# Division of the neighbourhood and banded probabilities by their sums, moved from VectorE to GpSimd

## The chip, the core and the metric

The kernel runs on one core of one Trainium2 chip. A core has TensorE (matrix products and transposes, results in PSUM), VectorE and ScalarE (element by element, in SBUF and PSUM), GpSimd (element by element, in SBUF) and SyncE, which issues DMA transfers. The engines run their own instruction lists side by side and wait for each other by semaphores. The metric is the device time of one execution in microseconds (us), lower is better.

## What is computed

Two transformer blocks in sequence over 512 tokens and 16 meta tokens of width 1024, in float32. The first has a feed-forward part, a mixer of stick-breaking attention and a recurrent part, and a second feed-forward part. The second block has a feed-forward part, three attention mixers side by side, a gated merge and a feed-forward part. The change touches two of these three mixers:

```python
# neighborhood_attention, 8 heads, a grid of 64 columns, meta keys always visible
p = jax.nn.softmax(jnp.concatenate([sm, s], axis=-1), axis=-1).astype(v.dtype)
p_nb = p[..., N_META:].reshape(bsz, H, GRID_W, wr, GRID_W)
return (jnp.einsum("bhcm,bmhd->bchd", p[..., :N_META], vm)
        + jnp.einsum("bhcxy,bxyhd->bchd", p_nb, v_nb))

# window_gqa, 8 query heads, 2 key heads, |i-j| <= 128, one sink logit per head
def sink_softmax(s, sink):
    m = jnp.maximum(jnp.max(s, axis=-1, keepdims=True), sink)
    e = jnp.exp(s - m)
    return e / (jnp.sum(e, axis=-1, keepdims=True) + jnp.exp(sink - m))
```

The third one (differential attention over all positions) has its own normalisation, which is left as it is.

## The kernel before

Nearly all of the time goes into products of weights and activations on TensorE, each in three passes (high by high, low by high, high by low part). The stage that matters here is `pe_mixers`, `act_mixers` and `dve_mixers`: attention of the second block.

**Units.** `mixer_units` lists 48 units: 16 of kind a (differential, 4 heads by 4 blocks of 128 queries), then 32 that alternate b (neighbourhood) and c (banded): `(b, p, i), (c, p, i)` for 4 head pairs p and 4 query blocks i. A b or c unit treats two heads x = 0, 1. Its probabilities of one head are 16 meta columns and 128 per key block: 272 columns for b and for c with i = 0 and 3, 400 columns for c with i = 1 and 2 (`blocks_of`). They lie in the tile P, of which six slots go round, two for a unit (`p_slot`), so a unit's slots are taken again by the unit three places on.

**Order.** `mixer_order` makes each engine's list. In round r an engine does, for each of its steps, the unit that lies so many places back:

```python
STEPS = {"PE": [(3, "turn"), (4, "values"), (0, "scores")],
         "ACT": [(3, "pt"), (1, "exp"), (5, "square"), (5, "yh")],
         "DVE": [(5, "out"), (1, "soft"), (2, "join"), (5, "yl")]}
```

For a b or c unit the steps follow on each other like this:
- scores (TensorE, L2825): four products for the two heads into PSUM, with 256 or 384 key columns and 16 meta columns.
- soft (VectorE, `dve_soft`, L2896 for b, L2906 and L2913 for c): a custom instruction that adds the bias to the scores, writes them negated into P and keeps the minimum in STAT. For c a small sum for the sink follows (L2917).
- exp (ScalarE, L2850): exponential in place in P, with the sum over the columns into STAT; for c also that of the sink (L2853).
- join (VectorE): for c the sink is added to the sum (L2951), then the reciprocal of both sums (L2954, semaphore a_inv), and two instructions that multiply the probabilities of each head by it (L2957, semaphore a_scl).
- turn (TensorE, L2777 and L2781): the transposes of P into PSUM, one of the meta columns and four or six of the key blocks. It waits for the unit's a_scl.
- pt (ScalarE, L2839 or L2841, L2844): copies them to SBUF. values (TensorE, L2796 and L2801): products with the values.
- yh, yl (ScalarE L2867 and L2870, VectorE L2973 and L2978): once per head pair, high and low part of the result, out of PSUM.

VectorE's list in a round with softmax of a c unit is thus L2906, L2913, L2917, then the join of the b unit before it; in the other kind of round L2896, then the join of the c unit before it. `mixer_counts` works out at which count of a semaphore each event of each unit stands.

**GpSimd** has a list of its own, `pool_program`: sums of squares (`pool_squares`), products in the recurrent part, fills and some DMA transfers (`pool_project_2`). Semaphore names of the second block go on counting on semaphores of the first (`GOES_ON`), so that the order of instructions shows a_inv as s_rho, a_scl as s_bonus, a_sum as s_sb_scan and a_exp as s_sb_keep.

Of the kernel before, what the change touches and what calls it, by code (L numbers as in the profile page):

```python
# [21 lines left out]
ALU = mybir.AluOpType  # L22
# [158 lines left out]
class Weights:  # L181
# [57 lines left out]
    def order_loads(self, dram):  # L239
# [13 lines left out]
        for i, item in enumerate(self.items):  # L253
# [20 lines left out]
            else:  # L274
# [17 lines left out]
       "lt", "half", "pm", "corner", "ks", "rs", "solved", "sa", "updated", "outs", "grown", "state", "yb",  # L292
       "y_hi", "y_lo",        "rowc", "lam",
              "hank0", "hank1", "rpb0", "rpb1", "rpb2", "bias",
       "v_moved", "v_turn", "a_min", "a_sink", "a_sq", "f_scl", "pad"])


GOES_ON = {"m1": ("lora", 8), "m2": ("knorm", 5), "gated": ("rkb", 4), "a_z": ("sb_z", 24),
# [70 lines left out]
def mixer_order(units, engine):  # L369


    return [(units[r - late], step) for r in range(len(units) + 5) for late, step in STEPS[engine]
            if 0 <= r - late < len(units)]


def mixer_counts(units):


    count, made = {}, {}

    def event(name, *keys):
        made[name] = made.get(name, 0) + 1
        for key in keys:
            count[name, key] = made[name]

    for u, step in mixer_order(units, "PE"):
        kind, h, i = u
        heads = kind in ("a", "b", "c")
        if step == "scores" and kind == "a":
            event("a_z", (u, 0))  # L390
        if step == "scores" and heads:
            event("a_z", (u, 1))
        if step == "turn":
            event("a_turn", u)
        if step == "values" and heads:
            event("a_val", u)
    for u, step in mixer_order(units, "ACT"):
        kind, h, i = u
        heads = kind in ("a", "b", "c")
        if step == "pt" and heads:  # L400
            event("a_pt")
            event("a_pt", u)
        if step == "exp" and heads:
            event("a_exp", (u, 0))
            event("a_exp", (u, 1))
            if kind == "c":
                event("a_sexp", u)
        if step == "square" and kind == "a":
            event("a_sq", u)
        if step == "yh" and kind in ("b", "c") and i == 3:  # L410
            event("yh", (4 if kind == "b" else 8) + h)
    for u, step in mixer_order(units, "DVE"):
        kind, h, i = u
        if step == "out" and kind == "a":
            event("a_y", u)
        if step == "soft" and kind in ("a", "b", "c"):
            if kind in ("a", "c"):
                event("a_min", (u, 0))
                event("a_min", (u, 1))
            event("a_sum", (u, 0))  # L420
            event("a_sum", (u, 1))
            if kind == "c":
                event("a_sink", u)
        if step == "join" and kind in ("a", "b", "c"):
            if kind == "c":
                event("a_den", u)
            event("a_inv", u)
            if kind == "a":
                event("a_nl", u)
            else:  # L430
                event("a_scl")
            event("a_scl", u)
        if step == "yl" and kind in ("b", "c") and i == 3:
            event("yl", (4 if kind == "b" else 8) + h)
    return count


def build(nc, dram, out):
    ctx = ExitStack()
    with ctx:  # L440
        S = {name: ctx.enter_context(nc.semaphore("s_" + name)) for name in SEMAPHORES}
# [365 lines left out]
        units = mixer_units()  # L807
        count = mixer_counts(units)
# [183 lines left out]
        def pool_squares(e, q, s, R, end=DT):  # L992
            for k in range(1, end):
                slot, _ = tmp_of["sq", s, k]
                q.wait_ge("sq", DT * s + k + 1)
                q.wait_ge("acc", ACC_BASE[s] + k - 1)
                e.tensor_tensor(tcols(ACC, R), tcols(ACC, R), tcols(TMP[:, slot, :], R),
                                ALU.add).then_inc(S["acc"], 1)
# [1698 lines left out]
        def p_slot(u):  # L2697
            return 2 * place_of[u] % 6

        def probs(u, x):  # L2700

            kind, h, i = u
            if kind == "a":
                return P[:, p_slot(u) + x, :]
            total = NM + 128 * blocks_of(u)
            return P[:, p_slot(u):p_slot(u) + 2, :].rearrange("p a n -> p (a n)")[:, x * total:(x + 1) * total]
# [25 lines left out]
        def stat(u, field, x, n=1):  # L2732
            return STAT[:, place_of[u] % 6, field, x:x + n]
# [25 lines left out]
        def pe_mixers(e, q):  # L2759
# [3 lines left out]
            for u, step in mixer_order(units, "PE"):  # L2763
                kind, h, i = u
                heads = kind in ("a", "b", "c")
                if step == "turn" and heads:
                    slot, n = p_slot(u), blocks_of(u)
                    q.wait_ge("a_scl", count["a_scl", u])
                    q.wait_ge("a_pt", 2 * place_of[u])
                    if kind == "a":  # L2770
                        e.transpose(PS[0:NM, 5, 384:512], P[:, slot, 0:NM], cst("ident"))
                        for y in range(n):
                            last = e.transpose(PS[:, 4, 128 * y:128 * y + 128],
                                               P[:, slot, NM + 128 * y:NM + 128 * y + 128], cst("ident"))
                    else:
                        both = P[:, slot:slot + 2, :].rearrange("p a n -> p (a n)")
                        e.transpose(PS[0:2 * NM, 5, 384:512], both[:, 128 * n:128 * n + 2 * NM], cst("ident"))  # L2777
                        for x in range(2):
                            for y in range(n):
                                bank, c = (4, 2 * x + y) if kind == "b" else (4 + x, y)  # L2780
                                last = e.transpose(PS[:, bank, 128 * c:128 * c + 128],  # L2781
                                                   probs(u, x)[:, parts_of(u, x)[0]][:, 128 * y:128 * y + 128],
                                               cst("ident"))
                    last.then_inc(S["a_turn"], 1)
# [139 lines left out]
        def dve_mixers(e, q):  # L2924
# [3 lines left out]
            for u, step in mixer_order(units, "DVE"):  # L2928
                kind, h, i = u
# [17 lines left out]
                if step == "join" and kind in ("b", "c"):  # L2947
                    q.wait_ge("a_exp", count["a_exp", (u, 1)])
                    if kind == "c":
                        q.wait_ge("a_sexp", count["a_sexp", u])  # L2950
                        e.tensor_tensor(stat(u, 2, 0, 2), stat(u, 2, 0, 2), stat(u, 3, 0, 2),  # L2951
                                        ALU.add).then_inc(S["a_den"], 1)
                        q.wait_ge("a_den", count["a_den", u])
                    e.reciprocal(stat(u, 4, 0, 2), stat(u, 2, 0, 2)).then_inc(S["a_inv"], 1)  # L2954
                    q.wait_ge("a_inv", count["a_inv", u])
                    for x in range(2):
                        e.tensor_scalar(probs(u, x), probs(u, x), stat(u, 4, x), None, ALU.mult).then_inc(S["a_scl"], 1)  # L2957
                if step == "yl" and u == units[-2]:
                    q.wait_ge("a_turn", 47)
                    q.wait_ge("a_sum", count["a_sum", (units[-1], 1)])  # L2960
# [8 lines left out]
                if step == "yl" and kind in ("b", "c") and i == 3:  # L2969
                    k = (4 if kind == "b" else 8) + h  # L2970
                    q.wait_ge("yh", count["yh", k])
                    if kind == "b":
                        e.tensor_tensor(YL[:, k, :].rearrange("p (r c) -> p c r", r=8),  # L2973
                                        out_bank_of(kind).rearrange("p (c r) -> p c r", r=8),
                                        YH[:, k, :].bitcast(F32).rearrange("p (r c) -> p c r", r=8),
                                        ALU.subtract).then_inc(S["yl"], 1)
                    else:
                        e.tensor_tensor(YL_C[:, h, :], out_bank_of(kind), YH[:, k, :].bitcast(F32),  # L2978
                                        ALU.subtract).then_inc(S["yl"], 1)

        def sync_strip(e, q, kind, h):
            s = h if kind == "a" else 4 + h
# [148 lines left out]
        def pool_program(e):  # L3131
            q = Waits(e, S)
            e.memset(FILLER, 1.0).then_inc(S["filled"], 1)
            q.wait_ge("load", 32)
            q.wait_ge("cst", 16)
            pool_squares(e, q, 1, FULL)
            pool_prepare(e, q)
            pool_breaking(e, q)
            pool_rwkv(e, q)
            pool_squares(e, q, 2, REAL, 4)  # L3140
            q.wait_ge("sq", 3 * DT)
            q.wait_ge("n_lo", 3 * DT)
            e.dma_start(X[:, :, 0:NM], dram["meta_2"]).then_inc(S["small"], 16)
            pool_to_meta(e, q)
            pool_squares(e, q, 5, FULL)
            pool_project_2(e, q)
            pool_squares(e, q, 6, REAL, 4)
            pool_squares(e, q, 7, REAL, DT - 1)

# [193 lines left out]
```

## Time and profile before

| | us |
|---|---|
| median of 3 runs | 2491.49 |
| lowest, highest | 2490.38, 2491.88 |
| span of the profiled execution | 2486.8 |
| TensorE busy | 2440.2 (98%) |
| VectorE busy | 1705.4 (69%) |
| ScalarE busy | 1081.3 (43%) |
| GpSimd busy | 98.2 (4%) |

The span is that of the instructions of one profiled execution; the times of the runs have what lies around it too. In the rows below a time is counted from the start of the span. In a timeline a row is: start, duration, engine, line of the kernel, operation, output<-input, shape, count, and in brackets how long the engine had been idle before and what ended that. PE is TensorE's products, PEld its weight loads, DVE is VectorE, ACT ScalarE, POOL GpSimd. A matmul's end is modelled, so a round on TensorE is best read from start to start.

### The profile page before, as it was taken

The page shows a single profiled execution, that of the slowest core. Times are in us where ns is not written, and L with a number is a line of the kernel's source. Part 1 is how long each engine was busy: PE and PEld are TensorE (multiplying, and loading weights), DVE is VectorE, ACT ScalarE, POOL GpSimd, SP SyncE. Part 2 cuts the span into 40 slices and gives each one's busy share as a digit, 9 for nine tenths or more (in the row PEclk, how much of TensorE's full clock was granted, in tenths as well). Part 3 has the DMA queues.
Part 4 walks back from the last instruction along what each step waited for, and adds up shares of the span by engine and source line. Part 5 has one row for each costly group of instructions (what it writes and reads, how often), then busy time and mean ns, then how long its engine had stood idle before and what let it go on. Part 6 is the DMA issues. An engine that isn't in the chain of part 4 may idle for free.

```text
span 2486.8 us, 49060 instructions
## 1 busy us (share of the span) xinstructions
PE 2440.2 (98%) x20460; PEld 2245.9 (90%) x20460; DVE 1705.4 (69%) x2926; ACT 1081.3 (43%) x1959; POOL 98.2 (4%) x108
## 2 busy tenths in 40 slices
PE   9999999999999999999999999999989999999998
PEld 7999999996887989898999999898867888989896
DVE  6878675646656879688879684242976445879694
ACT  5444343334434535356535253112874324535352
POOL 0000001000320000001000002000000000000001
PEclk8999999999999999998999999999999999999999
DMA  4233333220001333332233333232212333233322
GB/s 148 85 107 102 102 95 90 81 80 11 4 13 44 103 111 98 107 103 85 73 115 106 99 93 97 71 93 76 55 48 76 92 96 101 100 102 103 102 90 72
DMA packets 72379, 213.01 MB, mean 86 GB/s; under 512 B 12796, under 2 KB 20028, under 8 KB 72032
## 3 DMA queue, kind: packets, MB, share of 16 engines
q1 hardware_dynamic: 70496, 209.03, 26.7%
q8 instruction: 163, 2.67, 0.4%
q0 software_dynamic: 480, 0.73, 0.1%
q14 instruction: 56, 0.46, 0.1%
q10 hardware_dynamic: 1184, 0.12, 0.0%
HBM read 207.61 MB, written 2.20 MB: 84 GB/s over the span
## 4 chain that ended last, share of the span: by engine, by line
PE 87%; DVE 7%; ACT 4%; issue 2%; DVEq 0%; POOL 0%; ACTq 0%; POOLq 0%
PE PS L863 21%; PE PS L1398 20%; PE PS L1355 11%; PE PS L1356 11%; PE PS L1357 11%; DVE WL L948 1%; PE PS L1233 1%; ACT WH L936 1%; PE PS L1706 1%; PE PS L1707 1%; PE PS L1705 1%; PE PS L1319 1%; PE PS L2256 1%; DVE P L2888 1%; PE PS L2825 1%
## 5 line engine op out<-in xcount | busy, mean ns | idle before, releaser
L1355 PE MATMUL PS<-OPH,WH 128*128 128x256 f32 (+1 forms) x2112 | 606.4, 287 | 3.1 <-DVE OPL L1105 2.7
L1357 PE MATMUL PS<-OPH,WL 128*128 128x256 f32 (+1 forms) x2112 | 601.8, 285 | 0.0
L1356 PE MATMUL PS<-OPL,WH 128*128 128x256 f32 (+1 forms) x2112 | 600.2, 284 | 0.0
L936 ACT ACTIVATE WH<-WR 128x1024 fp32r<-128x1024 f32 (+2 forms) x277 | 275.5, 995 | 564.0 <-PE PS L863 272.6
L948 DVE TENSOR_TENSOR WL<-WR,WH 128x1024 fp32r<-128x1024 f32 (+2 forms) x277 | 318.7, 1151 | 191.1 <-ACT WH L936 191.0
L1355 PEld LDWEIGHTS PS<-OPH,WH 128*128 128x128 f32 x2112 | 403.5, 191 | 6.5 <-DVE OPL L1105 3.0
L1356 PEld LDWEIGHTS PS<-OPL,WH 128*128 128x128 f32 x2112 | 403.5, 191 | 2.1 <-issue 1.7
L1357 PEld LDWEIGHTS PS<-OPH,WL 128*128 128x128 f32 x2112 | 402.7, 191 | 0.0
L936 ACT ACTIVATE WH<-SUMS 128x512 fp32r<-128x512 f32 x352 | 211.1, 623 | 229.8 <-DVE SUMS L974 186.6
L948 DVE TENSOR_TENSOR WL<-SUMS,WH 128x512 fp32r<-128x512 f32 x352 | 234.1, 684 | 21.5 <-ACT WH L936 21.2
L863 PE MATMUL PS<-NHI,WH 128*128 128x264 f32 (+2 forms) x960 | 234.5, 309 | 1.5 <-ACT TMP L2623 1.0
L863 PE MATMUL PS<-NLO,WH 128*128 128x264 f32 (+2 forms) x960 | 232.9, 308 | 0.0
L863 PE MATMUL PS<-NHI,WL 128*128 128x264 f32 (+2 forms) x960 | 232.1, 307 | 0.0
L863 PEld LDWEIGHTS PS<-NHI,WH 128*128 128x128 f32 x960 | 154.9, 189 | 13.7 <-issue 1.6
L863 PEld LDWEIGHTS PS<-NLO,WH 128*128 128x128 f32 x960 | 156.1, 189 | 8.7
L863 PEld LDWEIGHTS PS<-NHI,WL 128*128 128x128 f32 x960 | 155.6, 189 | 8.3
L1398 PE MATMUL PS<-HH_A,WH 128*128 128x264 f32 (+1 forms) x572 | 152.3, 320 | 0.0
L1398 PE MATMUL PS<-HL_A,WH 128*128 128x264 f32 (+1 forms) x572 | 152.3, 321 | 0.0
L1398 PE MATMUL PS<-HH_A,WL 128*128 128x264 f32 (+1 forms) x572 | 151.9, 320 | 0.0
L1530 DVE TENSOR_TENSOR T<-PS,RT 128x528 f32<-128x528 f32 (+1 forms) x64 | 44.8, 699 | 148.1 <-PE PS L1398 148.1
L1398 PE MATMUL PS<-HH_B,WH 128*128 128x264 f32 (+1 forms) x476 | 127.1, 321 | 0.0
L1398 PE MATMUL PS<-HL_B,WH 128*128 128x264 f32 (+1 forms) x476 | 126.5, 321 | 0.0
(472 smaller groups left out, 4670.3 us busy)
## 6 DMA issues: line engine op xcount, KB each, us to landing
WR<-in_ffn_up SPq DMA_DIRECT2D x64, 512.0 KB, 3.9
WR<-in_ffn_down SPq DMA_DIRECT2D x64, 512.0 KB, 3.7
WR<-in_ffn_gate SPq DMA_DIRECT2D x56, 512.0 KB, 3.7
WR_MORE<-in_ffn_gate SPq DMA_DIRECT2D x32, 512.0 KB, 4.5
WR_MORE<-in_ffn_up SPq DMA_DIRECT2D x24, 512.0 KB, 4.4
WR<-in_ffn_down SPq DMA_DIRECT2D x32, 384.0 KB, 3.3
WR<-in_w_gate SPq DMA_DIRECT2D x24, 512.0 KB, 3.6
WR<-in_w_out SPq DMA_DIRECT2D x16, 512.0 KB, 3.6
```

The source lines that it names most:

```text
L863: last = e.matmul(bank, left[:, cols], right[:, a:b] if right.shape[1] == L else right, start=(kt == 0 and left is wh and right is hi), st ...
L936: e.activation(split_unit(i)[0][:, 0:w], src, ACT.Copy).then_inc(S["w_hi"], 1)
L948: e.tensor_tensor(lo[:, 0:w], src, hi[:, 0:w].bitcast(F32), ALU.subtract).then_inc(S["w_lo"], 1)
L1233: last = e.matmul(at[:, i:i + 1], data[:, a:a + 128], cst("ones", 128, 1), start=opens, stop=k == DT - 1, skip_group_check=True)
L1319: e.matmul(PS[:, 3, :], FILLER[:, 0:128], FILLER, start=True, stop=True, skip_group_check=True)
L1355: e.matmul(o, wh[:, at:at + 128], hi, start=k == 0 and s in (1, 2, 5), stop=False, skip_group_check=True)
L1356: e.matmul(o, wh[:, at:at + 128], lo, start=False, stop=False, skip_group_check=True)
L1357: last = e.matmul(o, wl[:, at:at + 128], hi, start=False, stop=k == 3, skip_group_check=True)
L1398: last = e.matmul(bank, left[:, cols], right[:, a:b], start=t == first and left is wh and right is hi, stop=t == end - 1 and left is wl, s ...
L1530: e.tensor_tensor(tcols(t, R), pcols(pair_of["down", f, c, m][0], R), tcols(RT, R), ALU.mult).then_inc(S["d_t"], 1)
L1705: e.matmul(o, NHI[:, kt, a:a + 128], wh[:, c], start=kt == 0, stop=False)
L1706: e.matmul(o, NHI[:, kt, a:a + 128], wl[:, c], start=False, stop=False)
```

## The change

The two multiplications leave VectorE's join for the kinds b and c and are made by GpSimd, in a new loop over the units, `pool_mixers`, which stands in GpSimd's list behind `pool_project_2` and ahead of the sums of squares. It waits for each unit's reciprocal. They count on a new semaphore, shared, for which the turn of a b or c unit now waits; a units keep a_scl.

```diff
-       "v_moved", "v_turn", "a_min", "a_sink", "a_sq", "f_scl", "pad"])
+       "v_moved", "v_turn", "a_min", "a_sink", "a_sq", "f_scl", "pad", "shared"])
@@ mixer_counts
             if kind == "a":
                 event("a_nl", u)
+                event("a_scl", u)
             else:
-                event("a_scl")
-            event("a_scl", u)
+                event("shared")
+                event("shared", u)
@@ pe_mixers
-                    q.wait_ge("a_scl", count["a_scl", u])
+                    scaled = "a_scl" if kind == "a" else "shared"
+                    q.wait_ge(scaled, count[scaled, u])
@@ dve_mixers
                     e.reciprocal(stat(u, 4, 0, 2), stat(u, 2, 0, 2)).then_inc(S["a_inv"], 1)
-                    q.wait_ge("a_inv", count["a_inv", u])
-                    for x in range(2):
-                        e.tensor_scalar(probs(u, x), probs(u, x), stat(u, 4, x), None, ALU.mult).then_inc(S["a_scl"], 1)
@@ new
+        def pool_mixers(e, q):
+            for u in units:
+                if u[0] == "a":
+                    continue
+                q.wait_ge("a_inv", count["a_inv", u])
+                for x in range(2):
+                    e.tensor_scalar(probs(u, x), probs(u, x), stat(u, 4, x), None, ALU.mult).then_inc(S["shared"], 1)
@@ pool_program
             pool_project_2(e, q)
+            pool_mixers(e, q)
             pool_squares(e, q, 6, REAL, 4)
```

VectorE's list before, from the softmax of the first 384-column c unit (ISA rows are the custom instruction and the read of its minimum) to the join of the b unit and the next softmax (line numbers after the change are two higher):

```order
L2913 ISA P,STAT<-PS,HANK,STAT 128x384 [waits s_a_min]
L2913 ISA STAT 128x1
L2917 TENSOR_TENSOR STAT<-STAT,SM 128x2 [waits s_sb_scan]
L2954 RECIPROCAL STAT<-STAT 128x2 [waits s_sb_keep]
L2957 TENSOR_SCALAR P<-P,STAT 128x272 [waits s_rho]
L2957 TENSOR_SCALAR P<-P,STAT 128x272
L2896 ISA P,STAT<-PS,BIAS 128x272 [waits s_rpb2,s_sb_turn,s_sb_z]
```

The same place after the change:

```order
L2915 ISA P,STAT<-PS,HANK,STAT 128x384 [waits s_a_min]
L2915 ISA STAT 128x1
L2919 TENSOR_TENSOR STAT<-STAT,SM 128x2 [waits s_sb_scan]
L2956 RECIPROCAL STAT<-STAT 128x2 [waits s_sb_keep]
L2898 ISA P,STAT<-PS,BIAS 128x272 [waits s_rpb2,s_sb_turn,s_sb_z]
```

The reciprocal is the last of the join now, and the next softmax stands right behind it.

GpSimd's list after the change, around the new loop's start; before, the row behind the fill of BIAS was the first sum of squares:

```order
L2682 MEMSET PT 128x2x128 [waits s_w_used]
L2683 MEMSET BIAS 128x3x32
L2986 TENSOR_SCALAR P<-P,STAT 128x272 [waits s_rho]
L2986 TENSOR_SCALAR P<-P,STAT 128x272
L2986 TENSOR_SCALAR P<-P,STAT 128x272 [waits s_rho]
```

Each pair waits for its unit's reciprocal (s_rho), the 32 pairs in the order of the units.

TensorE's list before, one round (transposes, values, scores) and the start of the next:

```order
L2777 MATMUL PS<-CST,P 32x128 [waits s_sb_pt,s_bonus]
L2781 MATMUL PS<-CST,P 128x128 x4
L2796 MATMUL PS<-PT,VMB 128x128 [waits s_rk]
L2801 MATMUL PS<-PT,VC 64x128 x4
L2825 MATMUL PS<-QK_128 128x384 [waits s_sb_scan]
```

And after:

```order
L2779 MATMUL PS<-CST,P 32x128 [waits s_sb_pt,s_shared]
L2783 MATMUL PS<-CST,P 128x128 x4
L2798 MATMUL PS<-PT,VMB 128x128 [waits s_rk]
L2803 MATMUL PS<-PT,VC 64x128 x4
L2827 MATMUL PS<-QK_128 128x384 [waits s_sb_scan]
```

Nothing moves on TensorE; the turn waits for GpSimd's semaphore in place of VectorE's. Values and scores still stand behind it.

## Rows read from the trace of the kernel before

**Rows 1.** The page's first part: engine, busy us (share of the span), instructions.

```profile
PE 2440.2 (98%) x20460; PEld 2245.9 (90%) x20460; DVE 1705.4 (69%) x2926; ACT 1081.3 (43%) x1959; POOL 98.2 (4%) x108
```

**Rows 2.** Timeline of two rounds, TensorE's first transpose (L2777) and VectorE.

```profile
1800.01 0.28 PE L2777 MATMUL PS<-CST,P 128*32 128x128 f32 x1
...
1801.05 0.17 DVE L2954 RECIPROCAL STAT<-STAT 128x2 f32<-128x2 f32 x1
...
1802.45 0.28 PE L2777 MATMUL PS<-CST,P 128*32 128x128 f32 x1
...
1802.57 0.23 DVE L2906 CUSTOM_DVE_ANT_0 P<-PS,HANK,NSINK 128x16 f32<-128x16 f32 x1 [0.69 <-PE PS L2825]
...
1803.89 0.16 DVE L2954 RECIPROCAL STAT<-STAT 128x2 f32<-128x2 f32 x1
...
1804.08 0.63 DVE L2957 TENSOR_SCALAR P<-P,STAT 128x272 f32<-128x272 f32 x2
```

**Rows 3.** Timeline of a round with a 384-column c unit, the same engines.

```profile
1787.53 0.28 PE L2777 MATMUL PS<-CST,P 128*32 128x128 f32 x1
...
1789.23 0.16 DVE L2954 RECIPROCAL STAT<-STAT 128x2 f32<-128x2 f32 x1
...
1790.11 0.28 PE L2777 MATMUL PS<-CST,P 128*32 128x128 f32 x1 [0.29 <-DVE P L2957]
```

**Rows 4.** The scaling's line L2957: count, ns min/median/max, first and last start, shapes.

```profile
L2957 DVE TENSOR_SCALAR P<-P,STAT x64: 353/361/429, 1783.9 to 1870.7; 128x272 f32<-128x272 f32 x48, 128x400 f32<-128x400 f32 x16
```

**Rows 5.** Timeline behind the end of a head pair, VectorE and TensorE's next transpose.

```profile
1812.07 0.69 DVE L2978 TENSOR_TENSOR YL_C<-PS,YH 128x512 fp32r<-128x512 f32 x1 [0.49 <-ACT YH L2870]
...
1813.59 0.17 DVE L2954 RECIPROCAL STAT<-STAT 128x2 f32<-128x2 f32 x1
...
1814.80 0.28 PE L2777 MATMUL PS<-CST,P 128*32 128x128 f32 x1
```

**Rows 6.** Timeline of GpSimd: fills and additions of different widths.

```profile
398.52 0.58 POOL L2009 MEMSET CHANNELS<- 128x576 f32 x1 [1.65 <-PE PS L863]
...
520.20 1.22 POOL L2128 MEMSET RENEW<- 128x1344 f32 x1 [119.25 <-PE PS L1905]
...
641.59 0.72 POOL L2417 TENSOR_TENSOR SMALL<-NB,CST 128x256 f32<-128x256 f32 x1 [2.73 <-PE PS L2256]
642.45 0.73 POOL L2417 TENSOR_TENSOR TMP<-NB,CST 128x256 f32<-128x256 f32 x1
...
775.21 1.41 POOL L997 TENSOR_TENSOR ACC<-ACC,TMP 128x512 f32<-128x512 f32 x1 [45.04 <-ACT TMP L990]
```

**Rows 7.** Timeline: VectorE hands over to GpSimd, and GpSimd to TensorE.

```profile
617.32 0.69 DVE L2365 TENSOR_TENSOR NB<-PS,CST 128x512 f32<-128x512 f32 x1 [0.33 <-PE PS L2206]
...
618.17 0.72 POOL L2417 TENSOR_TENSOR SMALL<-NB,CST 128x256 f32<-128x256 f32 x1 [11.19 <-DVE NB L2365]
...
2468.90 1.29 POOL L997 TENSOR_TENSOR ACC<-ACC,TMP 128x512 f32<-128x512 f32 x1 [4.29 <-ACT TMP L990]
2470.25 0.52 PEld L1624 LDWEIGHTS PS<-CST,ACC 128*128 128x128 f32 x4 [0.19 <-POOL ACC L997]
```

**Rows 8.** Timeline of the last unit: its reciprocal and its first transpose.

```profile
1870.18 0.17 DVE L2954 RECIPROCAL STAT<-STAT 128x2 f32<-128x2 f32 x1
...
1871.06 0.28 PE L2777 MATMUL PS<-CST,P 128*32 128x128 f32 x1 [0.16 <-DVE P L2957]
```

**Rows 9.** Windows: busy us of PE, PEld, DVE, ACT, POOL; granted clock; DMA.

```profile
1785.00:1870.00 85.00, 77.18 (x733) 61.65 (x731) 64.46 (x308) 62.54 (x208) 0.00 (x0) 0.96 0.19 49
...
1834.00:1841.00 7.00, 6.89 (x36) 5.08 (x37) 4.55 (x21) 2.66 (x8) 0.00 (x0) 0.51 0.12 39
```

**Rows 10.** Timeline: an addition on GpSimd while VectorE runs a two-input one.

```profile
637.58 0.69 DVE L2377 TENSOR_TENSOR TU<-TU,CST 128x512 f32<-128x512 f32 x1
...
637.67 1.19 POOL L2417 TENSOR_TENSOR TMP<-NB,CST 128x256 f32<-128x256 f32 x1
```

## The prediction

> **What bounds the kernel now.** First the page's busy shares and its chain: TensorE is busy 2440.2 of 2486.8 us and GpSimd 98.2 us [rows 1], so only what makes TensorE wait longer, or less, can move the time. The change touches one stage alone, the 32 neighbourhood (b) and banded (c) units between about 1782 and 1872 us. Over 1785 to 1870 TensorE is busy 77.18 of 85.00 us, VectorE 64.46, ScalarE 62.54, GpSimd nothing, at a mean granted clock of 0.96 [rows 9]. So TensorE sets the pace there too, but with little to spare around it, and the timeline has to be read for how much.
>
> In that stage each engine goes through the units in turn. A TensorE round is the transposes of unit u-3 ("turn"), the value products of u-4 and the scores of u. The scores start VectorE's softmax part of u, behind which stands "join" of u-1: a reciprocal of the sums, then two scalings of the probabilities. They let TensorE's next turn start. I count everything from the start of a turn.
>
> A free round is 2.44 us of TensorE work: the turn of 1800.01 is followed by the one of 1802.45 without a wait [rows 2]. VectorE's part of a round has two kinds:
> - X: softmax of a c unit, then join of a b unit. With the 256-column c unit the softmax starts 0.12 us after the turn and the reciprocal ends at 1804.05, 1.60 us after it; two scalings follow, and VectorE had waited 0.69 us for the scores [rows 2]. The next turn could start about 2.3 us after the last one, so TensorE does not wait. With the 384-column c unit the reciprocal ends at 1789.39, 1.86 us after the turn of 1787.53, and the next turn comes at 1790.11, after 2.58 us: 0.14 us late, with an idle TensorE ended by the scaling [rows 3].
> - Y: softmax of a b unit, then join of a c unit: the reciprocal ends at 1801.22, 1.21 us after its turn [rows 2], with 1.2 us left.
>
> So the scaling sits on a path with 0.1 us of slack in half of the X rounds and none in the other half. There are 16 X rounds, 8 of each width.
>
> **What is removed.** 64 VectorE instructions, 48 of 272 columns and 16 of 400, 353 to 429 ns each [rows 4]. A pair of 272 columns takes 0.63 us from first start to last end [rows 2]. That makes some 22 us of VectorE time free, and buys nothing by itself: VectorE's next softmax waits for TensorE's scores in these rounds, not for VectorE.
>
> **What is added.** 64 GpSimd scalings, in pairs, with a handoff at each side. GpSimd has nothing else to do here: the row before them in its queue is the fill of BIAS, and the sums of squares behind them belong to a later stage, so it is queued behind nothing and holds up nothing. What is queued behind the longer wait is TensorE's whole round.
>
> Handoffs: VectorE's NB ends at 618.01 and the GpSimd instruction that waits for it starts at 618.17, 0.16 us; GpSimd's ACC ends at 2470.19 and TensorE's load starts at 2470.25, 0.06 us. Together 0.22 us [rows 7].
>
> One scaling: the trace has no GpSimd instruction with one tensor read and one written, so I bound it. Below, a fill, which only writes: 0.58 us for 576 columns and 1.22 us for 1344, so 0.83 ns a column and 0.10 fixed, which gives 0.33 us for 272. Above, an addition, which reads two: 0.72 us for 256 and 1.41 us for 512 columns, 2.70 ns a column, which gives 0.76 us for 272 and 1.08 for 400. Two additions behind each other have 0.14 us between them [rows 6]. A scaling reads one and writes one, between the two, and neither row is nearer; I take the middle, 0.55 us for 272 and 0.76 us for 400 (fill 0.43). A pair is then 2 x 0.55 + 0.14 = 1.24 us, for 400 columns 1.66. From the reciprocal's end to the next turn it takes H = 0.22 + 1.24 = 1.46 us instead of 0.72.
>
> **The sum.** X with 256: 1.60 + 1.46 = 3.06 against 2.44, 0.62 us more. X with 384: 1.86 + 1.46 = 3.32 against 2.58, 0.74 more. Y with 400 columns: 1.21 + 0.22 + 1.66 = 3.09 from its turn, also over 2.44, but it costs nothing more: a late turn delays the scores behind it, and these feed the turn after the next, so that of two rounds in succession one pays; two rounds take 2.44 plus the larger of the two latencies. The next larger is X's each time.
>
> Three times, where a head pair ends, VectorE also makes the low part of the output (YL_C) ahead of a Y round, and that round starts late: its reciprocal ends at 1813.76 and the next turn comes at 1814.80 [rows 5]. With 0.22 + 1.66 = 1.88 it would come at 1815.64, 0.84 later, 0.10 beyond the 0.74 that the X round before has already cost. Three times: 0.3 us.
>
> At the end, the last unit's reciprocal ends at 1870.35 and its turn starts at 1871.06 [rows 8]; all that follows up to the gates hangs on it: 1.46 - 0.71 = 0.75 us.
>
> 8 x 0.62 + 8 x 0.74 + 0.3 + 0.75 = 11.9 us. After this stage TensorE is the bound again and gives nothing back. Against the profiled execution that is 2486.8 + 11.9 = 2498.7 us of span; the median of the runs lies 4.7 us above that span, so 2491.5 + 11.9 = **2503.4 us**.
>
> **Rivals.**
> Not slower: GpSimd scales at the rate of its fills and with no gap. H = 0.22 + 0.66 = 0.88: X with 256 costs 1.60 + 0.88 - 2.44 = 0.04, with 384 0.16, the end 0.17: 1.8 us, 2493.3 us, within what can be told from no change (0.2%, 5 us). The point that decides: 8 (H - 0.84) + 8 (H - 0.72) + (H - 0.71) = 17H - 13.2 reaches 5 us at H = 1.07, a pair of 0.85 us. For it: one read stream may cost no more than none. Against it: each scaling also fetches its factor per partition, and the addition costs over three times the fill. The Trainium skill ("GPSIMD Engine Reference", 4.1 Engine selection) says that two-input operations are about twice as slow there as on VectorE and one-input ones roughly at line rate; by that this rival would hold. The trace shows the first half (0.72 us for 256 columns) and nothing for the second.
>
> Two-read rate: the scaling costs what the addition does. Pair 1.66, H = 1.88: X 1.04 and 1.16, the three ends of head pairs 0.32 more each (2.52 us from 1813.76), the last one 1.17: 8 x 1.04 + 8 x 1.16 + 1.0 + 1.2 = 19.8 us, 2511.3 us.
>
> The clock: TensorE's granted clock was 0.51 over 1834 to 1841, some rounds behind the end of the second head pair; those 7 us did the work of about 3.5. That alone takes the mean of the 85 us to 0.96, so it was 1.0 in all the rest, behind the two other ends too [rows 9]. With more idle time in every second round, two more such stretches are possible: up to 7 us on top, around 2509 us. For it: the waits get longer. Against it: two of the three ends left the clock alone.
>
> Contention: an addition on GpSimd took 1.19 instead of 0.73 us while VectorE ran one with both inputs in SBUF [rows 10]. If VectorE's softmax instruction of the next unit, which runs while GpSimd scales, did the same, a scaling would take 1.01 us, a pair 2.16, H = 2.38: 17 x 2.38 - 13.2 + 0.3 = 27.6 us, 2519 us. Against it: that instruction reads PSUM and one SBUF operand. By the Trainium skill ("SBUF — State Buffer", Who interferes with whom) a VectorE instruction with at most one SBUF input outside its two-port modes does not contend with GpSimd; by that this rival falls away, and it leaves contention only at the end, where VectorE's NHI and NLO instructions run.
>
> A gain would need a pair plus its handoffs under 0.72 us, below two fills alone (0.66) with handoffs; only a low-clock stretch that happens not to occur could then bring some 2 us.
>
> **How the numbers follow.** Forecast (one scaling of 272 columns between 0.40 and 0.70 us, so H from 1.16 to 1.76 and 2498 to 2508 us) 0.57; fill rate 0.15; two-read rate 0.13; clock on top 0.08; contention 0.05; other 0.02. The range 2495 to 2514 leaves out the lower half of the fill case, contention and the clock on top of the dearer cases, under 0.2 together. Slower by over 0.2%: forecast, two-read, clock, contention and a little of the fill case, 0.84; within 0.2%: 0.13; faster 0.03.
>
> **What would show it.** In the profile after: GpSimd busy about 98 + 48 x 0.55 + 16 x 0.76 = 137 us; TensorE's first transpose of a unit idle before it in every X round, ended by GpSimd's P, about 10 us more in total; turns at distances of 2.44 and about 3.1 or 3.3 us in alternation; VectorE idle for longer before its softmax; the stages before and after of the same length; the gates start some 12 us later. I am wrong if a scaling lasts under 0.4 us (then TensorE hardly waits), if turns come late in both kinds of round, or if the low clock lasts longer than 7 us in this stage.

## The result, and the profile after

The changed kernel takes 2512.39 us (median of 4 runs, 2511.45 to 2516.51) against 2490.94 us before: 1.0094 times, 95% interval 1.0082 to 1.0106. It is slower by some 22 us. The forecast was 2503.4 us: the right direction, and about half of the size.

The page after. Columns are busy us, share of the span, instructions:

```profile
span 2509.4 us, 49060 instructions
...
PE 2444.1 (97%) x20460; PEld 2247.0 (90%) x20460; DVE 1685.9 (67%) x2862; ACT 1080.8 (43%) x1959; POOL 164.1 (7%) x172
```

Beside [rows 1], VectorE lost 19.5 us and 64 instructions, GpSimd gained 65.9 us and 64 instructions. The forecast had GpSimd at 137 us. The line of the new instructions, with shortest, median and longest duration in ns:

```profile
L2986 POOL TENSOR_SCALAR P<-P,STAT x64: 952/964/1287, 1783.7 to 1892.0; 128x272 f32<-128x272 f32 x48, 128x400 f32<-128x400 f32 x16
...
  DVE STAT L2956: 93.5, 27
...
  PEld PS L2779: 24.2, 22
  PE PS L2779: 21.6, 20
```

A scaling of 272 columns lasts 0.95 to 0.97 us in 47 of 48 cases (the last one of all 1.13), one of 400 columns 1.28 or 1.29; [rows 4] had 0.35 to 0.43 us on VectorE. TensorE's first transposes now wait 21.6 us for them. Before, they waited 2.5 us for the scalings on VectorE (the same view of L2957):

```profile
  PE PS L2777: 2.5, 6
```

One X round after, with a 256-column c unit, the counterpart of [rows 2]; the timeline of TensorE's first transpose (L2779 now), the reciprocal (L2956) and GpSimd:

```profile
1802.75 0.28 PE L2779 MATMUL PS<-CST,P 128*32 128x128 f32 x1
...
1804.11 0.16 DVE L2956 RECIPROCAL STAT<-STAT 128x2 f32<-128x2 f32 x1
1804.36 1.90 POOL L2986 TENSOR_SCALAR P<-P,STAT 128x272 f32<-128x272 f32 x2 [1.67 <-DVE STAT L2956]
...
1806.32 0.28 PE L2779 MATMUL PS<-CST,P 128*32 128x128 f32 x1 [1.06 <-POOL P L2986]
...
1808.76 0.28 PE L2779 MATMUL PS<-CST,P 128*32 128x128 f32 x1
```

The reciprocal ends at 1804.27, 1.52 us after the turn ("turn" always means the start of a unit's first transpose); GpSimd starts 0.09 us later, works 1.90 us on the pair without a gap, and the turn comes 0.06 us behind it: 2.05 us from the reciprocal to the turn, where the forecast had 1.46. The next distance, 1808.76 - 1806.32, is 2.44 us again: every second round pays, as forecast.

The chain of waits there, from the reciprocal ahead of one late turn to the start of the softmax ahead of the next; each piece is start, us, what:

```profile
1804.11 0.17 DVE STAT L2956
1804.28 0.08 issue
1804.36 1.91 POOL P L2986 x2
1806.27 0.04 issue
1806.32 0.28 PE PS L2779
1806.60 0.44 PE PS L2783 x4
1807.04 0.22 PE PS L2798 x2
1807.26 0.81 PE PS L2803 x12
1808.07 0.78 PE PS L2827 x8
1808.85 0.03 issue
1808.88 0.23 DVE P L2908
```

This is the circle that now sets the pace of the stage: one TensorE round, the softmax, the reciprocal, both scalings, and only then the next late turn. In between lies the turn that is on time.

The stage by a window, in the columns of [rows 9]:

```profile
1782.00:1894.00 112.00, 86.00 (x777) 68.64 (x775) 49.09 (x264) 65.22 (x219) 66.13 (x64) 0.92 0.14 40
```

The granted clock over the stage went from 0.96 [rows 9] to 0.92. Taken in windows of 1 us, it was low (0.5) for 17.1 us in four stretches, against 6.8 us in one before. From the first turn of a b unit to the turn of the last c unit it is 107.58 us (1785.65 to 1893.23) against 86.28 (1784.78 to 1871.06 [rows 8]): 21.3 of the 22.6 us by which the span grew. The first turn comes 0.87 us later too, since the first scalings stand ahead of it.

### The profile page after: what moved, and what is told of

It reads as the page before. It is cut to its first block, busy times and chain, and to the rows that moved or that the text cites. A ratio compares the mean times of both kernels' runs of the same rounds, so it can differ in the third digit from the quotient of the medians.

```text
span 2509.4 us, 49060 instructions
## 1 busy us (share of the span) xinstructions
PE 2444.1 (97%) x20460; PEld 2247.0 (90%) x20460; DVE 1685.9 (67%) x2862; ACT 1080.8 (43%) x1959; POOL 164.1 (7%) x172
## 4 chain that ended last, share of the span: by engine, by line
PE 86%; DVE 7%; ACT 4%; issue 2%; POOL 1%; DVEq 0%; ACTq 0%; POOLq 0%
PE PS L864 20%; PE PS L1399 20%; PE PS L1356 11%; PE PS L1357 10%; PE PS L1358 10%; DVE WL L949 1%; POOL P L2986 1%; ACT WH L937 1%; PE PS L1707 1%; PE PS L1708 1%; PE PS L1706 1%; PE PS L1320 1%; PE PS L1234 1%; PE PS L2257 1%; DVE P L2890 1%
## 5 line engine op out<-in xcount | busy, mean ns | idle before, releaser
L949 DVE TENSOR_TENSOR WL<-SUMS,WH 128x512 fp32r<-128x512 f32 x352 | 234.6, 686 | 21.9 <-ACT WH L937 21.6
L998 POOL TENSOR_TENSOR ACC<-ACC,TMP 128x528 f32<-128x528 f32 (+1 forms) x26 | 39.3, 1511 | 1401.2 <-ACT TMP L991 1401.2
```

The costliest lines, as they stand in the source:

```text
L949: e.tensor_tensor(lo[:, 0:w], src, hi[:, 0:w].bitcast(F32), ALU.subtract).then_inc(S["w_lo"], 1)
```

## The experiments

My theory after the result: the time from the reciprocal to the turn is the whole cost, it went from 0.72 to 2.05 us because of what the scaling takes on GpSimd, and of two rounds one pays. Rivals: each scaling pays for itself in its own round; the handoffs over a third engine cost, not the instructions; VectorE's work beside it slows GpSimd; the low clock carries a good part.

The table has all kernels but the one in which the forms of instruction are timed by themselves. "Turns" is the time from the first to the last of the 32 turns of the profile, of one execution each; "low" is the time at half clock in the stage. The kernel before was measured again beside each series: 2490.94 us beside the change, 2490.53 beside the next four rows, 2489.94 beside "the change, waits filled" and "before, three waits filled", and 2490.29 beside the other three. Differences are taken within a series.

| kernel | median us | to before (95% interval) | turns us | low us |
|---|---|---|---|---|
| before | 2489.9 to 2490.9 | | 86.28 | 6.8 |
| the change | 2512.4 | 1.0094 (1.0082 to 1.0106) | 107.58 | 17.1 |
| b units alone | 2515.15 | 1.0093 (1.0078 to 1.0108) | 108.84 | 23.9 |
| c units alone | 2505.27 | 1.0055 (1.0039 to 1.0072) | 102.74 | 10.2 |
| one head each | 2495.82 | 1.0022 (1.0012 to 1.0033) | 94.20 | 10.2 |
| one multiplication for both heads | 2495.52 | 1.0020 (1.0011 to 1.0030) | 92.13 | 6.8 |
| one head each, as a multiplication | 2490.46 | 1.0005 (0.9995 to 1.0014) | 88.07 | 6.8 |
| the change, waits filled | 2509.67 | 1.0074 (1.0059 to 1.0089) | 105.10 | 0.0 |
| b units alone, waits filled | 2504.54 | 1.0060 (1.0046 to 1.0074) | 101.03 | 0.0 |
| before, three waits filled | 2487.87 | 0.9992 (0.9983 to 1.0002) | 83.84 | 0.0 |
| the same, second series | 2487.47 | 0.9990 (0.9981 to 0.9999) | 83.81 | 0.0 |

### Half of the change: b units, c units

```diff
 # mixer_counts, pe_mixers: the turn of the other kind waits for a_scl again (left out here)
 # pool_mixers
-                if u[0] == "a":
+                if u[0] != "b":          # the other kernel: != "c"
 # dve_mixers, join: VectorE keeps the other kind
+                    if kind != "b":
+                        q.wait_ge("a_inv", count["a_inv", u])
+                        for x in range(2):
+                            e.tensor_scalar(probs(u, x), probs(u, x), stat(u, 4, x), None, ALU.mult).then_inc(S["a_scl"], 1)
```

> GpSimd scales the b units only, VectorE the c units as before. Theory (latency, one of two rounds pays): with 2.05 us from the reciprocal's end to the next turn, as in the profile after, the X rounds pay 8 x (1.60 + 2.05 - 2.44) + 8 x (1.86 + 2.05 - 2.58) = 20.3 us, nearly all of the change's 21.5 us, so about 2511 us. Rival (each scaling pays for itself, in every round): half of it, about 2502 us.

> GpSimd scales the c units only. Theory: the Y rounds, which had 1.2 us left, pay alone: 8 x (1.21 + 2.05 - 2.44) + 8 x (1.21 + 0.15 + 2.57 - 2.58) + 1.5 = 18.9 us, about 2510 us, so that this and the b half sum to some 39 us where both together cost 21.5. Rival (each pays for itself): about 11 us, 2502 us, and the two halves sum to the whole.

Measured: 24.6 us more for the b half and 14.7 for the c half, 39 us together, where the whole costs 21.5. The rival by which each scaling pays for itself falls: it needed halves of 11. That the sum also meets the theory's 39 is partly luck, for the halves missed it in opposite directions: the b half came out 4.3 us above its theory (2515.15 for 2511), which the section on the clock takes up, and the c half 4.2 us below (14.7 for 18.9). In the c half's profile the rounds into the three ends of head pairs fell from 4.42 to 3.61 us, which the theory did not count. The turns with the c units alone on GpSimd (the reading of the other half stands with its filled version, below):

```profile
1798.62 0.28 PE L2782 MATMUL PS<-CST,P 128*32 128x128 f32 x1
1802.59 0.28 PE L2782 MATMUL PS<-CST,P 128*32 128x128 f32 x1 [1.45 <-POOL P L2993]
1805.03 0.28 PE L2782 MATMUL PS<-CST,P 128*32 128x128 f32 x1
```

3.97 us for the round that waits for a pair of 400 columns (3.93 by the theory) and 2.44 for the next. In the changed kernel both kinds of round are late at times, and two rounds with 256-column softmax keep their sum:

```profile
1832.21 0.28 PE L2779 MATMUL PS<-CST,P 128*32 128x128 f32 x1 [0.71 <-POOL P L2986]
1835.08 0.28 PE L2779 MATMUL PS<-CST,P 128*32 128x128 f32 x1 [0.36 <-POOL P L2986]
1837.91 0.28 PE L2779 MATMUL PS<-CST,P 128*32 128x128 f32 x1 [0.32 <-POOL P L2986]
1841.17 0.28 PE L2779 MATMUL PS<-CST,P 128*32 128x128 f32 x1 [0.97 <-POOL P L2986]
```

2.83 + 3.26 = 6.09 us, which is 2.44 + 3.65, the free round and the late one. Waits in every round do not mean that every round pays.

### One head each

```diff
+                    e.tensor_scalar(probs(u, 0), probs(u, 0), stat(u, 4, 0), None, ALU.mult).then_inc(S["a_scl"], 1)   # VectorE
-                for x in range(2):
-                    e.tensor_scalar(probs(u, x), probs(u, x), stat(u, 4, x), None, ALU.mult).then_inc(S["shared"], 1)
+                e.tensor_scalar(probs(u, 1), probs(u, 1), stat(u, 4, 1), None, ALU.mult).then_inc(S["shared"], 1)   # GpSimd
 # left out: the counts, and the turn's wait, which is for both a_scl and shared now
```

> VectorE scales the first head of each b and c unit, GpSimd the second at the same time. Theory (the length of the GpSimd instructions is the cost): from reciprocal to turn 0.09 + 0.96 + 0.06 = 1.11 us, 8 x (1.60 + 1.11 - 2.44) + 8 x (1.86 + 1.11 - 2.58) + 0.4 = 5.7 us, 2497 us. Rival (what costs is the handoff over a third engine, or the low clock, whatever the length): more than half of the change's cost stays, over 2502 us.

Measured: 5.3 us more (2495.82 against 2490.53, interval 3.0 to 8.2 us), where 5.7 were expected; in the profile the turns take 7.9 us more. With about half of GpSimd's work gone, three quarters of the cost (by the medians) or two thirds (by the turns) are gone, so neither handoffs nor a third engine as such are the main price. The scaling itself was slower, though:

```profile
1800.02 0.16 DVE L2956 RECIPROCAL STAT<-STAT 128x2 f32<-128x2 f32 x1
...
1800.21 0.36 DVE L2958 TENSOR_SCALAR P<-P,STAT 128x272 f32<-128x272 f32 x1
...
1800.27 1.13 POOL L2987 TENSOR_SCALAR P<-P,STAT 128x272 f32<-128x272 f32 x1 [1.97 <-DVE STAT L2956]
...
1801.50 0.27 PE L2779 MATMUL PS<-CST,P 128*32 128x128 f32 x1 [0.41 <-issue]
```

1.13 instead of 0.96 us while VectorE scales the other head, in all 24 of that width (1127 ns is the shortest). From the reciprocal to the turn that makes 1.32 us in place of the expected 1.11, for which the prediction's line 17H - 13.2 gives 9.2 us; so the close hit of the median owes something to luck. In the changed kernel, where VectorE's custom instructions run beside the scalings, nothing of the kind happens: 952 ns shortest, 964 ns median. The Trainium skill ("SBUF — State Buffer", Who interferes with whom) counts a scaling on VectorE among the instructions that can take the port pair it shares with GpSimd; the trace agrees, with 0.17 us more for GpSimd's scaling.

### One multiplication for both heads

```diff
-                for x in range(2):
-                    e.tensor_scalar(probs(u, x), probs(u, x), stat(u, 4, x), None, ALU.mult).then_inc(S["shared"], 1)
+                ...   # both: the two slots of P as 128 x 2 x total, total = 16 + 128 per key block
+                by = stat(u, 4, 0, 2).unsqueeze(2).broadcast_to([128, 2, total])
+                e.tensor_tensor(both, both, by, ALU.mult).then_inc(S["shared"], 1)
```

> GpSimd scales both heads with one two-input multiplication whose second input repeats the two factors. Theory: at 2.70 ns a column, as its additions of the kernel before, 544 columns take 1.47 us in place of 1.90, H = 1.62, 17 x 1.62 - 13.2 = 14.3 us, about 2505 us, 7 us under the change. Rival (the form makes no difference, or the repeated operand costs as much as the factor of the scaling): 2512 us.

Measured: 5.0 us more (2495.52 against 2490.53). That is 16.5 us less than the change costs, where 7 less were expected. One instruction does both heads in 1.09 us, where the scaling takes 0.96 for one:

```profile
1800.50 0.16 DVE L2955 RECIPROCAL STAT<-STAT 128x2 f32<-128x2 f32 x1
...
1800.74 1.09 POOL L2988 TENSOR_TENSOR P<-P,STAT 128x544 f32<-128x544 f32 x1 [1.90 <-DVE STAT L2955]
...
1801.89 0.09 PEld L2778 LDWEIGHTS PS<-CST,P 128*32 128x32 f32 x1 [0.41 <-POOL P L2988]
1801.89 0.28 PE L2778 MATMUL PS<-CST,P 128*32 128x128 f32 x1 [0.31 <-POOL P L2988]
```

From the reciprocal's end (1800.66) to the turn 1.23 us, which is 17 x 1.23 - 13.2 = 7.7 us by the prediction's own line; the turns grew by 5.9. The columns are the same to the last one; what differs is the form of the instruction, and that there is one for two. The next run takes these two apart.

### The forms by themselves

```diff
+            for form in ("scalar_272", "scalar_400", "scalar_800", "number_272", "copy_272", "add_272", "spread_272",
+                         "spread_544"):
+                ...   # tensor_scalar with stat-like factor; with 1.5; tensor_copy; tensor_tensor of two tiles (ALU.mult);
+                      # tensor_tensor with one column repeated; with two columns repeated, 272 times each
```

> The kernel before, with 24 GpSimd instructions on a scratch tile in a stretch in which GpSimd idles (after the fill of VMB at 1612 us), three of each form. Theory (an instruction of this form costs this by itself): the scaling with a factor per partition takes 0.95 us for 272 columns and 1.28 for 400 here too; 800 columns 2.3 us. Rival (VectorE's softmax slows it in the changed kernel): 0.5 to 0.6 us for 272 here. The other forms tell what is dear: a plain number as factor, a copy, a multiplication of two tiles (0.76 by the additions), and one with a repeated factor, of 272 and of 544 columns.

This kernel was executed once. The third round of them, in GpSimd's timeline; the first row stands for the scaling of 272 columns alone, from a narrower window:

```profile
1636.08 0.96 POOL L2681 TENSOR_SCALAR ROWS<-ROWS 128x272 f32<-128x272 f32 x1
```

```profile
1641.38 0.89 POOL L2683 TENSOR_SCALAR ROWS<-ROWS 128x272 f32<-128x272 f32 x1
1642.33 0.41 POOL L2685 COPY ROWS<-ROWS 128x272 f32<-128x272 f32 x1
1642.83 0.78 POOL L2687 TENSOR_TENSOR ROWS<-ROWS 128x272 f32<-128x272 f32 x1
1643.69 0.64 POOL L2689 TENSOR_TENSOR ROWS<-ROWS 128x272 f32<-128x272 f32 x1
```

On a scratch tile, far from the stage, the scaling takes the same 0.96 us for 272 columns, 1.28 for 400 and 2.29 for 800, as the theory had it; with a plain number 0.89, so the factor per partition is not what is dear. A copy of the same columns takes 0.41: one read and one write are cheap, close to the fill rate (0.33). The multiplication of two tiles takes 0.78, as the additions said (0.76), and the one with a repeated factor 0.64. The scaling is the dearest of the five, dearer than the form that reads twice as much. So in the changed kernel too it is the form that makes it slow, and not what runs beside it.

These are the undisturbed rows. Six of the 24 took longer, and each of these began while VectorE ran L948, which makes the low part of the weights (two inputs in SBUF, 128x1024). The first scaling of 272 columns took twice its time:

```profile
1614.44 1.23 DVE L948 TENSOR_TENSOR WL<-WR,WH 128x1024 fp32r<-128x1024 f32 x1
1614.53 1.97 POOL L2681 TENSOR_SCALAR ROWS<-ROWS 128x272 f32<-128x272 f32 x1
```

### One head each, with the cheap form

```diff
-                e.tensor_scalar(probs(u, 1), probs(u, 1), stat(u, 4, 1), None, ALU.mult).then_inc(S["shared"], 1)
+                by = stat(u, 4, 1).broadcast_to([128, NM + 128 * blocks_of(u)])
+                e.tensor_tensor(probs(u, 1), probs(u, 1), by, ALU.mult).then_inc(S["shared"], 1)
```

> VectorE scales the first head, GpSimd the second with the multiplication by a repeated factor, 0.64 us for 272 columns by itself in the run on a scratch tile. Theory (only the time from reciprocal to turn counts): 0.09 + 0.64 + 0.06 = 0.79 us against 0.72 before, up to 0.17 more where it meets VectorE's scaling: 17 x 0.96 - 13.2 = 3.1 us at most, 0.5 us at least, so 2491 to 2493.5 us. Rival (any third engine on this path costs several us): as one head with the other form, over 2495 us.

Measured: 2490.46 against 2490.29 us, no difference that the runs tell (interval 1.2 us faster to 3.5 us slower); the turns of the profile take 1.8 us more. The path is almost as short as before, with GpSimd still in it:

```profile
1796.90 0.16 DVE L2956 RECIPROCAL STAT<-STAT 128x2 f32<-128x2 f32 x1
...
1797.09 0.84 DVE L2958 TENSOR_SCALAR P<-P,STAT 128x272 f32<-128x272 f32 x1
1797.13 0.64 POOL L2988 TENSOR_TENSOR P<-P,STAT 128x272 f32<-128x272 f32 x1 [2.25 <-DVE STAT L2956]
...
1797.98 0.28 PE L2779 MATMUL PS<-CST,P 128*32 128x128 f32 x1
```

The turn comes 0.92 us after the reciprocal. This time it is VectorE's scaling that is held up, 0.84 instead of 0.36 us (840 ns is the shortest of all), and GpSimd's instruction that keeps its length. The two overlap in the trace, but together they take 0.84 us, not much less than 0.36 + 0.64 one behind the other.

### The clock

A product of 512 columns with a constant tile, whose result is overwritten, stands on TensorE in each wait for a b unit's scaling and in each of the three waits for YL (the part of the head pair's result that VectorE takes out of PSUM, for which TensorE waits at the end of each pair but the last). In the two versions of the kernel before, only the three products in the waits for YL are there.

```diff
+                    q.wait_ge("a_pt", 2 * place_of[u])          # moved up from behind the wait for the scaling
+                    if kind == "b":
+                        e.matmul(PS[:, 4, :], cst("ident"), CST[:, 0:512], start=True, stop=True, skip_group_check=True)
                     q.wait_ge(scaled, count[scaled, u])
@@ values, ahead of the wait for the output bank
+                    if kind == "b" and h > 0 and i == 0:
+                        ...   # waits for a_sum, as the scores do that go to the same bank
+                        e.matmul(PS[:, score_banks(later)[0], :], cst("ident"), CST[:, 0:512], start=True, stop=True, ...)
```

> The changed kernel with one product of 512 columns on TensorE, whose result is overwritten, in each wait for a b unit's scaling, and one in each of the three waits for YL, so that TensorE stands still for less of them. Rival (the low clock carries a good part of the cost): the granted clock over the stage rises from 0.92 to 0.96 or more and 4 us or more come back, 2508 us or less. Theory (latency carries all, the low clock falls into the waits): less than 2 us either way, 2511 to 2514 us.

> The kernel before with one such product in each of the three waits for YL. If the low stretch of 7 us at 1834 comes from that wait and costs the 2.5 us by which its two rounds were longer (8.26 against 5.75 us), 2488.5 us; if it doesn't, 2491 us.

> GpSimd scales the b units only, with a product on TensorE whose result is overwritten in each wait for it and in the three waits for YL. Theory: the granted clock stays at 1.0, and the latency's 20.3 us stand alone on top of 2488 us, 2508 us; the b half without the products was at 2515 us, of which the low clock then carried the rest. Rival (the low clock costs nothing since it falls into waits): 2514 us or more.

> The kernel before with the products in the three waits for YL once more, on another day of the chip. If the 2.1 us of the first measurement are real, 2488 to 2489 us against 2490 to 2491; if they were noise, no difference.

The low stretches vanished in all four. The window of the stage, first the change filled, then the b half filled:

```profile
1782.00:1894.00 112.00, 99.39 (x838) 71.41 (x837) 50.77 (x267) 67.75 (x227) 66.44 (x64) 1.00 0.16 43
```

```profile
1782.00:1894.00 112.00, 103.94 (x870) 74.08 (x869) 65.14 (x312) 71.52 (x236) 30.52 (x32) 1.00 0.16 44
```

- The change went from 107.58 to 105.10 us of turns, and the kernel before from 86.28 to 83.84, by 2.5 and 2.4. So the clock's share in the difference is nothing: 21.3 us with it, 105.10 - 83.84 = 21.3 us without. The medians agree: 2509.67 - 2487.87 = 21.8 us between the filled kernels of one series, 21.5 us between the unfilled ones. 17.1 us at half clock cost the change no more than 6.8 us cost the kernel before. The filled change came out 1.3 us below the 2511 to 2514 us expected of it; by differences within the series it gained 1.7 us.
- With the b units alone the low clock cost 108.84 - 101.03 = 7.8 us of turns, 5.4 more than in the kernel before. This is why that half was no cheaper than the whole. Filled, it takes 2504.54 us, 3.5 under the 2508 expected. It costs 101.03 - 83.84 = 17.2 us of turns, and its turns stand as the theory has them, 3.92 and 2.44:

```profile
1798.59 0.28 PE L2785 MATMUL PS<-CST,P 128*32 128x128 f32 x1
1802.51 0.28 PE L2785 MATMUL PS<-CST,P 128*32 128x128 f32 x1 [0.35 <-POOL P L3002]
1804.95 0.28 PE L2785 MATMUL PS<-CST,P 128*32 128x128 f32 x1
```

Of the 3.1 us missing to 20.3, 2.2 lie at the three ends of head pairs, where the round behind the end fell from 3.17 to 2.43 us (the wait for YL_C is over before the late turn), and 0.2 in the last round. The other 0.7 is there because only 15 of the 16 X rounds lie between the first and the last turn; these paid 19.6 us.
- The kernel before with three such products is faster than before in both series, by 2.1 and 2.8 us (the second ran on another chip); the interval of the longer one excludes 1, that of the shorter one does not. It is the version that beats both kernels, by a thousandth.

Why did the low clock cost the b half 5.4 us more than the kernel before, and the whole change nothing more? The turns show where it was paid. In the b half five rounds grew by it: four from 2.43 or 2.44 us when filled to 4.00, 4.48, 3.43 and 4.40, and the last from 1.69 to 3.04, 7.9 us in all. In the change four rounds did: the first from 2.61 to 4.01, but the three behind the ends of head pairs take 3.57 or 3.58 us already when filled, because they wait for the c unit's scaling, and they went to 4.49, 3.49 and 3.84, so that the four give 2.5 us together. This fits a low clock that is partly hidden in a wait; no run moves the stretches one by one, so it is not shown.

## Why the prediction was right and wrong

**What bounds the stage, and what goes free:** right. VectorE's 20 us bought nothing; its idle time before the softmax of the c units went from 9.2 us in total (L2906) to 31.3 (L2908). TensorE remains the bound outside of the stage: the gates began again 22.2 us later than before (1899.38 against 1877.22).

**Place and shape of the cost:** right in the main. Where the turn is on time, the X round's reciprocal ends 1.52 to 1.59 us after it with a 256-column c unit and 1.86 with a 384-column one, as forecast; late turns stand in X rounds, 2.44 us in between, and of two rounds one pays. The handoffs were 0.09 + 0.06 = 0.15 us where 0.22 was taken. That X's latency is the larger of the two each time did not hold, though: by the theory behind the halves a Y round with 400 columns needs 3.93 us from its turn, more than the 3.65 and 3.91 of the X rounds, which fits the turns of c units that came late too. That was one of the prediction's own signs of being wrong, and the low clock for over 7 us was another; both came, but neither makes the main part of the miss.

**One scaling:** this step failed. The prediction bounded it by a fill from below (0.33 us) and by a two-input addition from above (0.76) and took the middle, 0.55; for 400 columns 0.76. It is 0.96 and 1.29 us, outside of both bounds, since the form with one input and a factor is slower on GpSimd than the one with two inputs. The argument "it reads one tile and writes one, so it lies between" measured the traffic and not the instruction: the copy, which has this traffic, takes 0.41. With the measured 2.05 us in place of 1.46, the prediction's own terms for the 16 X rounds give 8 x 1.21 + 8 x 1.33 = 20.3 us instead of 10.9; the stage took 21.3 us more from the first to the last turn, and the gates began 22.2 us later.

**The gap between two scalings** (0.14 us): not there, 1.90 us for a pair of 0.96 each; 0.14 us a pair too much, against 0.8 too little for the two scalings.

**The last unit:** counted as a term of its own beside the X rounds. It is the Y round behind an X round and falls under the rule of the pair: its distance grew from 1.90 to 2.24 us, 0.34, and not by 1.34.

**The rivals.** Fill rate: wrong by a factor of three. The Trainium skill ("GPSIMD Engine Reference", 4.1 Engine selection) calls one-input operations "roughly line-rate"; here the copy comes near that (0.41 us for 272 columns, where VectorE's scaling takes 0.36), and the scaling with 0.96 us does not. Two-read rate: its 2511.3 us nearly hit the result, yet with a scaling of 0.76 us where 0.96 was measured; it was not the case that came about, and its number came near by luck, for its scaling was too short and its gap and handoffs too long. Clock on top: more low stretches came, 17.1 us in all, and cost the change no more than the one before had cost. Contention with the softmax: absent, 0.95 to 0.97 us in all scalings of 272 columns but the last, which took 1.13 us beside NHI and NLO on VectorE.

**The numbers.** 2512.4 us lies in the range of 2495 to 2514, at its upper edge, and the change of 21.5 us is 1.8 times the forecast one. That the range held is luck: it reached so far up for the sake of the two-read rival, while the range of one scaling, 0.40 to 0.70 us, was missed.

## What to carry to other kernels

Before work is moved to an engine that has not yet run that form of instruction, its price is open upwards too: measure the form on a scratch tile in a stretch where the engine idles, it costs one run. What a free engine is worth is decided by the time from its input to whoever waits, not by its idle share: GpSimd was 96% idle and VectorE was relieved of 20 us, and neither fact said anything about the time. When two or more rounds are in flight between a wait and its cause, add latencies over the whole circle; the waits of single rounds neither add up to the loss nor predict it.

## What the runs showed of the hardware

- GpSimd, float32, 272 columns: copy 0.41 us, multiplication with a repeated factor 0.64, of two tiles 0.78, scaling with a number 0.89, scaling with a factor per partition 0.96; 400 columns 1.28, 800 columns 2.29. 544 columns as one multiplication with repeated factors take 1.09.
- VectorE's scaling and a GpSimd instruction can hold each other up: 1.13 instead of 0.96 us on GpSimd in one kernel, 0.84 instead of 0.36 us on VectorE in another. Begun beside the instruction that makes the low part of the weights on VectorE (L948), a GpSimd scaling took 1.97 instead of 0.96 us; beside its custom instructions of the softmax it kept 0.95 to 0.97.
- A single product of 512 columns in each of three waits of 1.4 us kept the granted clock at 1.0 in both profiles of a stage that otherwise had 6.8 us at half clock, and took 2.4 us off it.
